# A two-layer hybrid transformer on one core: the memory projection's opening rearranged, and the end of the second mixer cut into parts

## What is computed

```python
mkv = rmsnorm(mem, mem_norm_g) @ w_mem_kv            # once, for both layers
xn = rmsnorm(h, norm_mix_g[layer])
# layer 0, the S5 half: lam_bar = exp(lam*step), b_bar = ((lam_bar-1)/lam)*b, powers of lam_bar
# layer 1 (odd mixer): z = xn @ w_in
yc = rmsnorm(mlstm(...)) * sigmoid(c_o)              # 4 heads of 128
yd = moba_attention(q, k, v)                         # 4 heads of 128, block-sparse softmax
mix = concatenate([yc, yd]) @ w_out                  # 8 blocks of 128 rows of w_out
```

## Time and profile before

| | |
|---|---|
| median of 3 runs | 1253.91 us (1253.66 to 1254.07) |
| the profiled execution | 1253.44 us, of which its span 1251.7 us |
| PE busy | 1172.5 us (94%) |
| DVE, ACT, POOL busy | 706.2, 587.5, 358.8 us |
| mean granted TensorE clock | 0.979 |

### The profile page before, as it was taken

The page is one execution under the profiler, slowest core; times in us unless marked ns, Lnnn a source line. Parts: engine busy times, 40 slices in busy tenths (PEclk is TensorE's granted clock), DMA queues, the critical chain, the costliest instruction groups (busy, mean ns, idle before and its releaser), DMA issues.

```text
span 1251.7 us, 15333 instructions
## 1 busy us (share of the span) xinstructions
PE 1172.5 (94%) x5227; PEld 869.3 (69%) x5227; DVE 706.2 (56%) x1280; ACT 587.5 (47%) x1130; POOL 358.8 (29%) x311
## 2 busy tenths in 40 slices
PE   4999999999899799999899999979998997999996
PEld 2468876788667466666678877757887684666665
DVE  5893534320522688888744983771205216888887
ACT  2453246354723366665535364352546333566661
POOL 2024340564022021113136663253350220211120
PEclk9999999999999899999999999989998998999999
DMA  9433232376101799997232130022311008999963
GB/s 274 148 124 87 31 110 68 115 299 259 68 1 61 316 366 374 384 378 291 85 116 76 68 135 1 1 69 88 113 68 68 1 26 344 353 382 382 384 224 132
DMA packets 77643, 214.92 MB, mean 172 GB/s; under 512 B 23620, under 2 KB 24560, under 8 KB 65272
## 3 DMA queue, kind: packets, MB, share of 16 engines
q1 hardware_dynamic: 64688, 180.22, 39.1%
q0 software_dynamic: 10048, 28.92, 6.4%
q10 hardware_dynamic: 2840, 4.91, 1.1%
HBM read 187.90 MB, written 32.51 MB: 176 GB/s over the span
## 4 chain that ended last, share of the span: by engine, by line
PE 76%; DVE 13%; ACT 5%; issue 3%; DMA 1%; POOL 1%; DVEq 0%; POOLq 0%; ACTq 0%
PE bank L836 38%; PE bank L1166 7%; PE bank L1199 7%; PE bank L1171 6%; PE bank L1071 2%; PE bank L1112 2%; DMA E<-xs,idx 1%; DVE h L2321 1%; PE bank L1085 1%; PE bank L872 1%; PE bank L1015 1%; DVE E2r L2282 1%; PE bank L1222 1%; PE bank L1062 1%; PE bank L1340 1%
## 5 line engine op out<-in xcount | busy, mean ns | idle before, releaser
L675 POOL TENSOR_TENSOR wlo<-W,whi 128x512 fp32r<-128x512 f32 x176 | 254.5, 1458 | 469.8 <-ACT whi L1418 450.4
L1418 ACT ACTIVATE whi<-W 128x512 fp32r<-128x512 f32 x176 | 107.7, 633 | 245.5 <-PE bank L836 239.0
L836 PE MATMUL bank<-whi,xTr 128*128 128x512 f32 x480 | 192.2, 400 | 0.9 <-ACT E L1819 0.6
L836 PE MATMUL bank<-wlo,xTr 128*128 128x512 f32 x416 | 162.7, 391 | 0.0
L836 PEld LDWEIGHTS bank<-whi,xTr 128*128 128x128 f32 x480 | 90.7, 189 | 22.0 <-POOL wlo L675 1.7
L1171 PE MATMUL bank<-E4r,E1r 128*128 128x512 f32 x360 | 98.5, 422 | 0.0
L1199 PE MATMUL bank<-whi,E2r 128*128 128x512 f32 x256 | 90.5, 415 | 6.7 <-DVE E2r L2282 5.2
L1914 DVE TENSOR_TENSOR h<-bank,h 128x512 f32<-128x512 f32 x32 | 21.8, 692 | 131.3 <-PE bank L836 131.3
L836 PEld LDWEIGHTS bank<-wlo,xTr 128*128 128x128 f32 x416 | 78.7, 189 | 16.9 <-issue 1.2
L1171 PEld LDWEIGHTS bank<-E4r,E1r 128*128 128x128 f32 x360 | 67.5, 188 | 27.0 <-issue 7.4
L708 POOL COPY idx<-slots 128x1 uint32 (+1 forms) x30 | 5.5, 182 | 276.8 <-PE bank L1146 184.8
(11 more groups left out here) (485 smaller groups left out, 2433.5 us busy)
## 6 DMA issues: line engine op xcount, KB each, us to landing
E<-in_moe_w SPq DMA_DIRECT2D x48, 1024.0 KB, 10.2
W<-in_moe_w SPq DMA_DIRECT2D x32, 1024.0 KB, 9.8
xT<-in_moe_w SPq DMA_DIRECT2D x16, 1024.0 KB, 12.5
W<-in_od_w_in SPq DMA_DIRECT2D x7, 2048.0 KB, 8.7
ybuf<-E SPq DMA_DIRECT2D x26, 512.0 KB, 6.9
ybuf<-memV POOLq DMA_DIRECT2D x12, 1024.0 KB, 19.7
W<-in_w_mem_kv SPq DMA_DIRECT2D x4, 2048.0 KB, 8.5
W<-in_xa_wq SPq DMA_DIRECT2D x4, 2048.0 KB, 8.5
```

The costliest lines, as they stand in the source:

```text
L675: pool.tensor_tensor(wlo[s_ % RING][:, :], slot(name)[:, k, :], whi[s_ % RING][:, :].bitcast(F32), ALU.subtract).then_inc(S["w_lo"], 1)
L836: ins = pe.matmul(bank(u + t)[:, :], a, b, start=(k == 0 and n == 0), stop=(k == KT - 1 and n == 2))
L1418: act.activation(whi[s_ % RING][:, :], slot(name)[:, k, :], ACT.Copy).then_inc(S["w_hi"], 1)
```

## The change

- **Opening, loads.** Panel kv0 is issued second, before the S5 tensors. The 13 small vectors go behind panel kv3. The memory's gain vector is waited for by itself; POOL makes the identity first.
- **Opening, order.** PE turns the memory rows unscaled, at once; ACT shares the evacuation with DVE (gain only), and the memory norm is applied when ACT copies the results out (`scale=mem_rstd`). ACT squares the tokens before the sines. DVE scales the tokens before all combines and takes their low parts after the first. PE turns the tokens after kv1, then does kv2 and kv3, then bT.
- **Buffers.** E1 and E3 change roles in the first layer, so that the tokens' low parts and `s5Qn` don't share one.
- **End of the second mixer.** POOL squares as soon as both pairs of heads are out, in four parts, into E5 in place of E2; it multiplies by the gate before it needs the norm, and again in four parts by the norm. ACT, not DVE, scales head 3's probabilities. out10 and out11 go in block order 4, 5, 0, 1, 2, 3, 6, 7, and hh is turned behind the first block.

```diff
+        def block_of(name, k):
+            return (4, 5, 0, 1, 2, 3, 6, 7)[k] if name in ("out10", "out11") else k
...
             sp.dma_start(memtok, A["mem"][0].rearrange("(a p) d -> p a d", p=P)).then_inc(S["mem_in"], 16)
+            load_panel(0)
             for dst, src in s5_loads:
                 sp.dma_start(dst, src, allow_slow_non_contiguous=True).then_inc(S["s5_in"], 16)
-            load_panel(0)
...
                 sp.dma_start(B2[lo:lo + NS], B1[NS - lo:2 * NS - lo]).then_inc(S["s5_b2"], 16)
-            for dst, src in small:
-                sp.dma_start(dst, src, allow_slow_non_contiguous=True).then_inc(S["small_in"], 16)
             sp.dma_start(wsN, A["gm_ws"][0].rearrange("h t s -> t h s")).then_inc(S["wide_in"], 16)
             for p in range(2, first_of_layer1):
                 load_panel(p)
+                if p == pnum["kv3"]:
+                    for dst, src in small:
+                        sp.dma_start(dst, src, allow_slow_non_contiguous=True).then_inc(S["small_in"], 16)
...
+            p_(pool.memset(ident[:], 0.0))
+            select(ident[:], 0, [[-1, P]], 1, ALU.not_equal, 1.0)
+            pool.sem_inc(S["consts_ready"], 1)
             for dst, src in lam_loads:
                 pool.dma_start(dst, src).then_inc(S["lam_in"], 16)
...
-            await_filled(pool, first["dv"] + 3)
             taken_all(pool, "num0", 4)
             taken_all(pool, "num1", 4)
-            p_(pool.tensor_tensor(hsq, hh, hh, ALU.mult), "hh_sq")
+            for t in range(TT):
+                p_(pool.tensor_tensor(hsq[:, t, :], hh[:, t, :], hh[:, t, :], ALU.mult), "hh_sq")
+            for t in range(TT):
+                p_(pool.tensor_tensor(hh[:, t, :], hh[:, t, :], SO[:, t, :], ALU.mult))
             pool.wait_ge(S["hh_rstd"], 1)
-            h16 = spare_slot[:, 0:2048].rearrange("p (n d) -> p n d", n=16)
-            p_(pool.tensor_tensor(h16, h16, drec[:, 0:16].unsqueeze(2).broadcast_to([P, 16, P]), ALU.mult))
-            p_(pool.tensor_tensor(hh, hh, SO, ALU.mult), "hh_ready")
+            for t in range(TT):
+                h4 = hh[:, t, :].rearrange("p (n d) -> p n d", n=4)
+                p_(pool.tensor_tensor(h4, h4, drec[:, 4 * t:4 * t + 4].unsqueeze(2).broadcast_to([P, 4, P]), ALU.mult),
+                   "hh_ready")
...
+            pe.wait_ge(S["mem_in"], 32)
+            u = first["mg"]
+            fill(pe.transpose(bank(u)[:, 0:KT], rows[0:KT, :], ident[0:KT, 0:KT]), u)
             u = first["memT"]
-            for t in range(MT):
-                pe.wait_ge(S["xn_ready"], t + 1)
...
                 fill(ins, u)
                 u += 1
-            taken_all(pe, "memT", 4)
...
+                        if n == t == 0 and k % 2 == 0:
+                            taken(pe, first["memT"] + k // 2)
                         ins = pe.matmul(bank(u)[:, :], memnT[:, k, t * P:(t + 1) * P], slot(f"kv{n}")[:, k, :],
...
             memory_gemm(1)
+            transpose_gain_norm("mix_norm0")
             memory_gemm(2)
-            pe.wait_ge(S["s5_bb"], 1)
+            memory_gemm(3)
+            pe.wait_ge(S["s5_tables"], 1)
...
-            transpose_gain_norm("mix_norm0")
-            memory_gemm(3)
             split_gemm(first["s5u"], "ev2", by_k(xhi), by_k(xlo["ev"]), lambda k: taken(pe, first["mix_norm0"] + k),
...
-            for n in range(4):
+            def gated_turn(n):
                 u = first["ycT"] + n
                 claim(pe, u)
                 for t in range(TT):
+                    pe.wait_ge(S["hh_ready"], t + 1)
                     ins = pe.transpose(bank(u)[:, t * P:(t + 1) * P], hh[:, t, n * P:(n + 1) * P], ident[:])
                 fill(ins, u)
...
+                return [part[block_of("out10", k)] for k in range(KT)]
+            def mixed_ready(k):
+                b = block_of("out10", k)
+                taken(pe, first["ycT"] + b if b < 4 else first[f"mo{b - 4}"])
             for n in range(2):
-                split_gemm(out1_bank(n, 0), f"out1{n}", by_k(xhi),
-                           by_k(xlo["out1"])[4:] + by_k(xlo["out1"])[:4],
-                           lambda k: taken(pe, first["ycT"] + k if k < 4 else first[f"mo{k - 4}"]),
-                           between={} if n else {0: [(moba_out, 2)], 2: [(moba_turn, 3)], 4: [(moba_out, 3)]})
+                split_gemm(out1_bank(n, 0), f"out1{n}", mixed_blocks(by_k(xhi)),
+                           mixed_blocks(by_k(xlo["out1"])[4:] + by_k(xlo["out1"])[:4]), mixed_ready,
+                           between={} if n else {0: [(gated_turn, k) for k in range(4)], 1: [(moba_out, 2)],
+                                                 2: [(moba_turn, 3)], 4: [(moba_out, 3)]})
...
             act.activation(rho8, are, ACT.Exp, scale=float(LC)).then_inc(S["s5_exp"], 1)
+            squares("mix_norm0")
             act.wait_ge(S["s5_args"], 2)
-            act.wait_ge(S["consts_ready"], 1)
+            act.wait_ge(S["consts_ready"], 2)
...
-            squares("mix_norm0")
             root("mix_norm0")
-            copies("kv0", 0, 2, lambda n: memtok[:, n, 0:512])
-            copies("kv1", 0, 2, lambda n: memtok[:, n, 512:1024])
-            copies("kv2", 0, 2, lambda n: memV[:, n, 0:512])
-            for n in range(8):
...
-                evac(act.activation(E[1][:, 512 * n:512 * n + 512], bank(u)[:, :], ACT.Copy), u)
+            def mem_rstd(n):
+                return rstd[:, 0, n:n + 1]
+            act.wait_ge(S["mem_rstd"], 1)
+            copies("kv0", 0, 2, lambda n: memtok[:, n, 0:512], scale=mem_rstd)
+            copies("kv1", 0, 2, lambda n: memtok[:, n, 512:1024], scale=mem_rstd)
             norm("mix_norm0")
-            weights("ev2", 0, RING)
             taken(act, first["kv1"] + 1)
             for t in range(MT):
                 for n in range(4):
                     a_(act.activation(junk[:, 0:XD], memtok[:, t, n * XD:(n + 1) * XD], ACT.Square,
                                       accum_out=xmx[:, 4 * t + n:4 * t + n + 1]), "hd_sq")
-            copies("kv3", 0, 2, lambda n: memV[:, n, 512:1024])
+            copies("kv2", 0, 2, lambda n: memV[:, n, 0:512], scale=mem_rstd)
+            weights("ev2", 0, RING)
+            copies("kv3", 0, 2, lambda n: memV[:, n, 512:1024], scale=mem_rstd)
+            for n in range(8):
+                u = first["bT"] + n
+                await_filled(act, u)
+                evac(act.activation(E[3][:, 512 * n:512 * n + 512], bank(u)[:, :], ACT.Copy), u)
             weights_between("ev2", "ev1")
             act.wait_ge(S["hmean_ready"], 1)
...
+            def moba_probs(n):
+                for t in range(TT):
+                    act.wait_ge(S["sums_ready"], t + 1)
+                    act.activation(pm(n, t), pm(n, t), ACT.Copy, scale=xrec[:, 4 * n + t:4 * n + t + 1])\
+                        .then_inc(S["last_probs"], 1)
...
             moba_exp(3)
-            weights("out10", 0, RING)
+            weights("out10", 0, 2)
             moba_high(1)
+            weights("out10", 2, RING)
             moba_turn(2)
+            moba_probs(3)
             for n in range(4):
                 high_part(first["ycT"] + n, xhi[:, n, :])
...
-            rstd_of_tokens("mix_norm0")
+            dve.wait_ge(S["std_ready"], v.n["mean_ready"])
+            v(dve.reciprocal(rstd[:, n0, :], std[:, n0, :]))
+            for t in range(TT):
+                ts(h[:, t, :], h[:, t, :], rstd[:, NORMS["mix_norm0"], t:t + 1], None, ALU.mult).then_inc(S["xn_ready"], 1)
             combine(BB1, Fr, B1, Fi, B2)
+            norm("mix_norm0")
             combine(BB2, Fr, B2, Fi, B1, ALU.subtract)
             for j in range(LC):
                 combine(s5Qn[:, :, j, :], Lr[:, :, LC - 1 - j], BB1, Li[:, :, LC - 1 - j], BB2)
-            dve.nop().then_inc(S["s5_bb"], 1)
-            for t in range(TT):
...
-                    norm("mix_norm0")
                 combine(s5PP[:, :, k, :], Lr[:, :, k], C1, Li[:, :, k], C2)
-            dve.nop().then_inc(S["s5_pp"], 1)
+            dve.nop().then_inc(S["s5_tables"], 1)
...
-            dve.wait_ge(S["hh_sq"], 1)
-            v(dve.tensor_reduce(dsq[:, 0:16], v3(E[2], 16, 0, 2048), AX.X, ALU.add))
+            dve.wait_ge(S["hh_sq"], TT)
...
             moba_turn(1)
             dve.wait_ge(S["hstd_ready"], 4)
             dve.reciprocal(drec[:, 0:16], dstd[:, 0:16]).then_inc(S["hh_rstd"], 1)
+            moba_low(0)
             moba_max(3)
-            moba_low(0)
-            moba_probs(3)
+            for t in range(TT):
+                taken(dve, first["ms3"] + t)
+                dve.reciprocal(xrec[:, 12 + t:13 + t], xsum[:, 12 + t:13 + t]).then_inc(S["sums_ready"], 1)
             moba_low(1)
             moba_turn(2)
             for n in range(4):
```

More of the change, by code:

```diff
@@ L39, in uses_of_banks @@
 def uses_of_banks(layers):
-    steps = [("cols", 1), ("memT", 4), ("kv0", 2), ("ct", 2), ("kv1", 2), ("kv2", 2), ("bT", 8), ("mix_norm0", 8),
[1 row of a table removed]
```

(8 more changed lines are left out.)

106 lines of the change are left out of this document (57 added, 49 removed), and 2 rows, old and new, of the table steps.

## The result

The changed kernel takes **1236.51 us** (median of four runs, 1235.06 to 1237.83), the kernel before 1253.99 (1253.66 to 1254.55): a ratio of 0.9855, 95% interval 0.9842 to 0.9867, or 17.5 us less. 1240 was predicted, 1237 to 1243 at 0.50 and 1234 to 1246 around it, and faster at 0.92: the time lies inside the wide range and just outside the narrow one. The profiled execution took 1236.83 us, its span 1235.1 against 1251.7 us.

The account below looks back on a forecast made before the run. PE, busy 94% of the span, was taken as the bound, with losses in the opening and at the second mixer's end; 5 + 9 = 14 us off 1253.9 gave 1240 us, range 1237 to 1243 at 0.50.

Parts of the forecast that it names:

- Opening, 5 taken: Up to s5u's start: worked out as 6.6 us earlier, less 1.7 for a possible clock fall; 5 taken.
- Their chain: Opening: x lands at 30.2, squares to 34.5, small sines to 36.8, DVE to 43.1, tokens scaled by 46.0.
- the 1.7 us for the clock: Opening: price if PE's clock falls while it waits for the tokens, slowing their transposes; 1.7 us.
- The tokens' wait: Opening: PE, ready for the tokens at 42.0, mostly waits until they are scaled at 46.0.
- the work said to be hidden: Opening: DVE's combines, low parts, ACT's per-row scale, memory norm and small loads were to stay covered, costing nothing.
- End, 9 taken: Second mixer's end, last dv matmul to out10's end: 52.1 us falls to 39.9 to 44.1; 9 us gain taken.
- four squares, 3.6 us together: Second mixer's end: POOL's squares no longer wait for dv and end at 814.6 instead of 824.2.
- with `moba_low(0)` (0.7) now ahead: Second mixer's end: from head 1's copy at 823.7 to ACT's first high part at 828.7 to 829.8.
- The first block's wait: Second mixer's end: PE waits 1 to 2.2 us for out10's first weight block; lost clock 0 or 3.0.
- Both parts clean: Rival, chance 0.17: no slow clock in either part and x a little earlier, 8 + 11.5, about 1234 us.
- The clock that stays low through kv2: Rival, chance 0.10: slow transposes cost 3.3 and kv2 2.3 more, opening gives 1, end 10: 1244 us.
- Small loads as a bound: Rival, chance 0.04: small loads issued between kv3 and ev2 take about 24 us longer and slow the kernel: 1257 us.

Follow-up runs that it names:

- the eight traces of the table: Eight profiled executions with the new order of squares and sines and an early panel, including the changed kernel's; s5u starts at 78.71 to 82.73.
- The first trace: First profiled execution of the changed kernel, with no further edit: 1236.83 us, s5u starting at 78.90.
- opening_only: The kernel before with only the opening's edits: 1247.04 us, ratio 0.9922.
- whole_products: The changed kernel with POOL's squares, gate products and norm products each in one instruction instead of four: 1238.60 us, ratio 0.9876.
- small_first: The changed kernel with the thirteen small loads issued ahead of panels kv2 and kv3: 1239.69 us, ratio 0.9873.
- tokens_first: The changed kernel with the tokens' root, reciprocal and scaling ahead of the state-space sines on ACT and DVE: 1237.59 us, ratio 0.9860.

## Why the prediction was right

*Opening, 5 taken.* kv0 began at 12.2 for 11, which cost nothing, since the tokens decided, as forecast. Their chain came as worked out, from x through squares, small sines and DVE's 6.3 us to the scaling, each piece within 0.2 us. s5u came at 78.7 to 82.7 in the eight traces of the table, with 80.5 to 82 forecast. The first trace gained 8.2 because two terms came out well in it, which is luck: x was there at 28.8, not 30.2 (it was 29.7 in opening_only), and the 1.7 us for the clock were not due. In five of the eight traces the clock did fall, at 1.5 to 1.7 and once 2.8. The tokens' wait was put at 4.0 and was 1.1 to 4.0. Of the work said to be hidden, tables, low parts and small loads all were.

*End, 9 taken, 8.7 measured.* Full-clock work was 38.4 and is 38.3 (39.99 busy less 0.04 x 43.4). PE's wait for head 1's copy, 2.90, is gone; hh is off the path. Inside the sum some terms were off. POOL's pieces take 4.40 for the whole's 3.60 and 5.39 for 4.60, which the step "four squares, 3.6 us together" had left out. DVE's scaling of head 2 lost 2.9 us beside POOL, not 2: 4.9 with its reciprocals (808.13 to 813.06), where head 1's, alone, took 2.0. So head 1's copy came 1.3 us later than forecast (done at 816.9; 823.7 less the opening's 8.1 is 815.6). But that is hardly what made the first block late. The step that was wrong is the one from this copy to ACT's high part, "with `moba_low(0)` (0.7) now ahead": moba_low(0) isn't 0.7 us of work behind the copy, it waits for ACT's high part of head 0, and that for PE's output of head 0, which ends at 816.6 whatever the sum does. It begins 0.4 us after the copy is done. Of head 2's slow scaling only PE's wait of 0.53 stands in that path. whole_products agrees: there DVE waits the same 0.26, PE 0.34 in place of 0.53, and the first block's wait is 2.85 again. ACT's first high part thus came at 822.75, where 820.6 to 821.7 was forecast (828.7 to 829.8 less 8.1). The first block's wait was 2.85 and not 1 to 2.2, and the clock fell, at 1.6 and not at 3.0; the two errors nearly cancel.

*What of the end made the gain?* Undone one at a time, the order of blocks is worth 2.3 us, the pieces 0 and head 3's move to ACT 0. Some 6.4 us are left. The traces put them down to POOL's squares no longer waiting for dv, since the wait of 5.31 us that DVE had for them is gone and with it PE's for head 1's copy, and to the gate products ahead of the norm. That is argued, not shown: neither was undone singly, nor were moba_low(0) ahead of head 3's maxima and ACT's first two weight copies ahead of head 1's high part, so how these four share it stays open.

*The rivals.* "Both parts clean" would have been 1234; the first trace lies between it and the forecast. The clock that stays low through kv2 was not seen: kv2 and kv3 took 27.6 to 27.7 in every trace with the new opening. Small loads as a bound: small_first rules it out. What was forecast for no trace is the spread between executions: with one order of instructions s5u starts anywhere in 4 us, by x's landing and the clock at the tokens.

## What to carry to other kernels

When a wait of the critical engine is named "issue", look at which engine makes its next operand and ask what that one waited for: here it was a copy of 0.6 us queued behind an exponential, and moving it gave 3.5 us. When a stage is moved forward, list all that its results and its banks need, since removing the tokens' wait uncovered three waits for evacuations, 3.5 us together. When an engine's functions are reordered, look for the next one that relied on the table loaded last: tokens_first's turned up 60 us further on. And where TensorE still waits for a us or two, take the gain from several executions, not from one trace.
